# A hybrid attention and mixture-of-experts block on one core: two written orders of attention work replaced by two others

## The chip, the cores and the metric

The kernel runs on one core of one Trainium2 chip. The time is that of one execution on the device, in microseconds (us); several executions of the kernel before gave a median of 1522.29 us (1521.67 to 1523.18). Inside a core, TensorE multiplies and transposes, VectorE and ScalarE do elementwise work and copy results out of PSUM, GpSimd does small SBUF work, and SyncE issues most DMAs. In the profile they are PE (with PEld, its weight loads), DVE, ACT, POOL and SP.

## What is computed

Two layers on 256 tokens of width 1024. Each layer is an attention mixer with three kinds of heads, followed by a feed-forward part: a dense SwiGLU in layer 0, eight experts with two chosen for each token in layer 1.

```python
for layer in range(DEPTH):                                   # DEPTH = 2
    h = h + hybrid_mixer(rms_norm(h, attn_norm[layer]), ...)  # dsa, diff and mla heads, then @ w_out
    hn = rms_norm(h, ffn_norm[layer])
    if layer % 2 == 0:
        h = h + swiglu(hn, dense_w_gate[j], dense_w_up[j], dense_w_down[j])
    else:
        h = h + moe_ffn(hn, moe_router[j], moe_w_gate[j], moe_w_up[j], moe_w_down[j])
return rms_norm(h, final_norm)
```

In the mixer, "dsa" heads attend only to the 64 keys with the highest index score for each query. "diff" heads subtract one softmax from another, and "mla" heads work on keys and values that are expanded from a narrow latent.

## The kernel before

The 256 tokens are two tiles of 128 (t = 0 and 1). A float32 product is made of three passes over split operands: every weight part of 1024 columns is split into a high part by ScalarE (`split_hi`, L1293) and a low part by VectorE (`split_lo`, L1614), and TensorE runs high by high, high by low and low by high (`part_product`, L898).

The program has four stages after one another: attention of layer 0, `dense`, attention of layer 1, `experts`. In `dense` and `experts` the order is written in loops. In the two attention stages it comes from the two texts in `LISTS`. Each word is an item of work, and **every engine walks the same list** and issues its own share of each item (`attention` at L791 for GpSimd, L980 for TensorE, L1318 for ScalarE, L1754 for VectorE). An engine executes in the order in which it issues; between engines only semaphores hold. So a word's place decides what stands ahead of it on every engine that takes part. Nothing else plans the order: no costs, no due times.

The words that the later sections use:

- `X.t.i`, `OT.t.i`, `XF.t.i`: transposes of activations ahead of the input projections, the output projection and the feed-forward part. ScalarE and VectorE copy the result out, high and low.
- `SP.n`: the split of weight part n, four parts for each projection. Parts 0 to 19 belong to `PC`, `PA`, `PB`, `PI`, `PK`, parts 20 to 27 to the output projection, 28 to 30 to the first weights of the stage that follows. There are 7 buffers, so a split from part 7 on first waits until the projection that read part n - 7 is done (`part_free`, L473). A load into a ring slot waits until the slot's old parts are split.
- `PC`, `PA`, `PB`, `PI`, `PK` .t: input projections, 24 matmuls each. `C1`, `C2`, `CT`, `QC`, `KV`, `MQ`, `MK`: the mla latents' norm, their transposes and the expansion. `R.*`: rotary embedding on GpSimd.
- `U.kind.t.p`: logits of one pair of heads (TensorE, L973), their maximum (VectorE, L1718) and the exponential (ScalarE, L1414). For `U.idx`, the index heads, VectorE instead adds to the score (L1685, L1687). `CB`: the combination of a diff pair on VectorE (L1841 to L1844). `TP`, `O`: transposed probabilities, and the product with the values.
- `TK.t.r`: one of eight rounds that find the top 64 scores, all on VectorE (L1703, L1704), each on the result of the one before. `U.dsa` needs `TK.t.7`.
- `D1`, `D2`: the diff heads' norm. `WO.t.half`: the output projection, 24 matmuls, after all heads of tile t.
- `NF1`, `NF2`, `HS`, `RT`, `PL`, `GR` (layer 1): norm, split of the rows, router, places and the gather of rows for the experts. `GR.1.1` needs `HS.1.1`.
- `FL.n`: four transposes of the identity that nobody reads (`turn_identity`, L878). There are 16 in each list.

The list of layer 0 has 224 words, that of layer 1 has 240.

Of the kernel before, what the change touches and what calls it, by code (L numbers as in the profile page):

```python
# [38 lines left out]
C1.1 PA.0 PA.1 R.kr.0 CT.0 C2.1 SP.8 R.kr.1 FL.4 SP.9 QC.0.1 CT.1 SP.10 SP.11 KV.0.1 QC.0.0 KV.0.0 R.c.0 PB.0
MQ.0.0 MQ.0.1 MK.0.0 MK.0.1 KV.1.0 QC.1.1 QC.1.0 U.mla.0.3 SP.12 U.mla.0.2 KV.1.1 SP.13 R.c.1 CB.mla.0.3 PB.1  # L40
SP.14 MQ.1.1 SP.15 SP.16 R.a.0 MK.1.0 MK.1.1 CB.mla.0.2 U.mla.0.0 MQ.1.0 PI.0 SP.17 SP.18 SP.19 TP.mla.0.2
SP.20 SP.21 PI.1 TP.mla.0.3 PK.0 SP.22 U.mla.1.0 PK.1 R.i.0 KIT.0 SP.23 R.b.0 IT.0 O.mla.0.2 R.i.1 TP.mla.1.0
O.mla.0.3 R.a.1 U.idx.0.0 TP.mla.0.0 CB.mla.0.0 U.idx.0.1 U.idx.0.2 CB.mla.1.0 U.idx.0.3 BT.0 U.mla.1.2
U.mla.1.1 U.diff.0.2 KIT.1 CB.mla.1.2 CB.mla.1.1 FL.5 TK.0.0 O.mla.1.0 TK.0.1 O.mla.0.0 CB.diff.0.2 IT.1
TP.mla.1.2 U.diff.0.3 TP.mla.1.1 U.diff.0.1 TK.0.2 O.mla.1.2 CB.diff.0.3 TP.diff.0.2 U.mla.0.1 CB.diff.0.1
FL.7 O.mla.1.1 TK.0.3 TK.0.4 FL.2 TP.diff.0.3 O.diff.0.2 TK.0.5 U.idx.1.0 SP.24 R.b.1 AT.0 TP.diff.0.1
O.diff.0.3 CB.mla.0.1 U.idx.1.1 TP.mla.0.1 U.idx.1.2 U.idx.1.3 BT.1 U.diff.0.0 TK.0.6 U.diff.1.2 FL.12
CB.diff.0.0 O.diff.0.1 TK.1.0 CB.diff.1.2 O.mla.0.1 TK.0.7 TP.diff.0.0 U.dsa.0.0 U.dsa.0.1 O.diff.0.0 TK.1.1
TP.diff.1.2 CB.dsa.0.0 U.mla.1.3 D1.0 FL.13 TK.1.2 TP.dsa.0.0 FL.8 O.diff.1.2 FL.15 AT.1 TK.1.3 CB.mla.1.3
TK.1.4 CB.dsa.0.1 TP.dsa.0.1 U.diff.1.0 U.diff.1.1 O.dsa.0.0 FL.14 TP.mla.1.3 D2.0 CB.diff.1.0 U.diff.1.3  # L50
O.dsa.0.1 FL.3 CB.diff.1.1 TP.diff.1.0 O.mla.1.3 TK.1.5 OT.0.1 OT.0.0 TK.1.6 TP.diff.1.1 O.diff.1.0 TK.1.7
U.dsa.1.0 U.dsa.1.1 CB.diff.1.3 O.diff.1.1 WO.0.0 TP.diff.1.3 TP.dsa.1.0 O.diff.1.3 TP.dsa.1.1 D1.1 SP.25
# [6 lines left out]
TP.mla.0.1 U.mla.0.2 SP.15 CB.mla.0.1 MQ.1.1 TP.mla.0.0 SP.16 MK.1.1 PI.0 SP.17 SP.18 CB.mla.0.3 O.mla.0.1
U.mla.1.3 CB.mla.0.0 PI.1 TP.mla.0.3 SP.19 SP.20 SP.21 CB.mla.0.2 PK.0 SP.22 U.mla.1.0 PK.1 O.mla.0.0  # L60
O.mla.0.3 R.i.0 R.i.1 SP.23 CB.mla.1.3 TP.mla.1.3 R.b.0 TP.mla.0.2 IT.0 KIT.0 U.mla.1.2 O.mla.0.2 U.idx.0.0
TP.mla.1.0 O.mla.1.3 U.idx.0.1 TP.mla.1.2 KIT.1 U.idx.0.2 U.idx.0.3 TK.0.0 R.b.1 CB.mla.1.2 CB.mla.1.0 IT.1
# [2097 lines left out]
```

How the kernel before makes its waits and increments, by code:

```python
        def job(eng, key):  # L406
            eng.wait_ge(job_done, JOB[key] + 1)
            return work[JOB[key] % WBANKS]
# [1 line left out]
        def emptied(eng, key):  # L411
            eng.wait_ge(evacuated[JOB[key] % WBANKS], JOB[key] // WBANKS + 1)
# [7 lines left out]
        def arrived(eng, use, rounds=0):  # L421
            eng.wait_ge(slot_full[use % RING], rounds + 16 * (use // RING + 1))
# [50 lines left out]
        def part_free(eng, part, shift=0):  # L473
            for layer in range(DEPTH):
                i = (part - LAYER_PART[layer]) // 4
                if 0 <= i < len(SPLIT_SLOTS):
                    name = SPLIT_SLOTS[i]
                    keys = [(layer, name, t) if name in PROJ else (layer, "WO", t, int(name[2])) for t in range(T)]
                    eng.wait_ge(job_done, max(JOB[key] for key in keys) + 1)
                    return
            eng.wait_ge(part_used, shift + used_up(part))
# [76 lines left out]
        def roped_by(eng, layer, key):  # L559
            eng.wait_ge(roped, layer * len(ROPES[0]) + ROPES[layer].index(("R", *key)) + 1)
# [39 lines left out]
            def freed(use):  # L600
                if use in FREE:
                    sp.wait_ge(*FREE[use])
# [70 lines left out]
            def chunk_split(half, n):  # L673
                sp.wait_ge(lo_done, n * 4 + (first_part(half) + 4))
# [21 lines left out]
            def store(first):  # L697
                for t in range(T):
                    sp.wait_ge(out_ready, first + t + 1)
                    sp.dma_start(out[0, t * P:(t + 1) * P, :], final[:, t, :]).then_inc(stored, 16)
```

## Time and profile before

| | us |
|---|---|
| median of 3 executions | 1522.29 |
| the profiled execution | 1522.29 |
| its span, first to last instruction | 1520.5 |
| attention of layer 0, first projection to first dense product | 10.7 to 150 |
| attention of layer 1, first projection to first expert product | 389.2 to 539.2 |
| PE busy, share of the span | 1493.6 (98%) |
| DVE busy | 1255.1 (83%) |
| ACT busy | 1041.4 (68%) |

The busy time of PE counts pipelined matmuls and runs on through short waits, so the share is read together with the order of time. The granted clock is the share of TensorE's full clock that it was given; 1.00 is 2.4 GHz, and its other level is 0.5, 1.2 GHz. Over the span it was 0.992.

### The profile page before, as it was taken

What the parts mean: (1) busy time and instruction counts of PE and PEld (TensorE: products, weight loads), DVE (VectorE), ACT (ScalarE), POOL (GpSimd) and SP (SyncE); (2) the same over time, 40 slices, a digit from 0 to 9 for tenths busy, and PEclk for the clock granted to TensorE, in tenths of its full rate; (3) what the DMA queues carried; (4) which work ended last, traced back from release to release, by engine and by line L of the source; (5) the groups of instructions that cost most, each with busy time, mean ns of one, the idle gap of its engine ahead of it and who ended that gap; (6) DMA issues with size and microseconds to landing.
All of it is one profiled execution on the core that took longest, in us unless ns stands there. A gap on an engine that the chain in (4) does not pass through costs nothing.

```text
span 1520.5 us, 19069 instructions
## 1 busy us (share of the span) xinstructions
PE 1493.6 (98%) x7182; PEld 1245.2 (82%) x7182; DVE 1255.1 (83%) x1544; ACT 1041.4 (68%) x1362; POOL 98.1 (6%) x173
## 2 busy tenths in 40 slices
...
GB/s 283 202 56 56 241 189 199 171 212 127 125 202 57 57 282 384 387 363 364 351 362 364 359 363 363 365 363 377 342 370 362 365 367 365 362 371 375 363 371 107
DMA packets 181823, 431.11 MB, mean 284 GB/s; under 512 B 3937, under 2 KB 10465, under 8 KB 181729
## 3 DMA queue, kind: packets, MB, share of 16 engines
...
## 4 chain that ended last, share of the span: by engine, by line
PE 95%; DVE 2%; ACT 1%; issue 1%; DMA 0%; POOL 0%; POOLq 0%; ACTq 0%; SPq 0%; DVEq 0%
PE pair L903 51%; PE work L903 33%; PE work L875 3%; PE pair L973 2%; PE pair L875 2%; PE work L1047 1%; PE work L890 1%; PE work L1181 1%; DVE arena L1687 0%; PE work L1195 0%; PE work L1196 0%; ACT w_hi L1272 0%; DMA ring<-in_w_in 0%; DVE w_lo L1619 0%; DVE nmax L1718 0%
## 5 line engine op out<-in xcount | busy, mean ns | idle before, releaser
L1619 DVE TENSOR_TENSOR w_lo<-ring,w_hi 128x1024 fp32r<-128x1024 f32 (+3 forms) x810 | 961.6, 1213 | 191.2 <-ACT w_hi L1272 177.3
L1272 ACT ACTIVATE w_hi<-ring 128x1024 fp32r<-128x1024 f32 (+3 forms) x810 | 840.4, 1053 | 310.6 <-PE pair L903 140.3
L903 PE MATMUL pair<-w_hi,hnT_hi 128*128 128x512 f32 x672 | 265.1, 394 | 1.7 <-DVE hnT_lo L1986 0.9
L903 PE MATMUL pair<-w_hi,hnT_lo 128*128 128x512 f32 x672 | 262.0, 390 | 0.0
L903 PE MATMUL pair<-w_lo,hnT_hi 128*128 128x512 f32 x672 | 261.5, 389 | 0.0
L903 PE MATMUL work<-w_hi,hidT_hi 128*128 128x512 f32 x552 | 215.5, 390 | 2.6 <-DVE hidT_lo L1920 1.4
L903 PE MATMUL work<-w_lo,hidT_hi 128*128 128x512 f32 x552 | 214.9, 389 | 0.0
L903 PE MATMUL work<-w_hi,hidT_lo 128*128 128x512 f32 x552 | 214.8, 389 | 0.0
L903 PE MATMUL pair<-w_hi,xU_hi 128*128 128x512 f32 x448 | 177.1, 395 | 0.0
L903 PE MATMUL pair<-w_hi,xU_lo 128*128 128x512 f32 x448 | 174.8, 390 | 0.0
L903 PE MATMUL pair<-w_lo,xU_hi 128*128 128x512 f32 x448 | 174.3, 389 | 0.0
L903 PEld LDWEIGHTS pair<-w_hi,hnT_hi 128*128 128x128 f32 x672 | 126.2, 188 | 27.1 <-DVE hnT_lo L1636 1.2
L903 PEld LDWEIGHTS pair<-w_hi,hnT_lo 128*128 128x128 f32 x672 | 126.1, 188 | 26.8
L903 PEld LDWEIGHTS pair<-w_lo,hnT_hi 128*128 128x128 f32 x672 | 126.3, 188 | 25.2
L903 PEld LDWEIGHTS work<-w_hi,hidT_hi 128*128 128x128 f32 x552 | 103.7, 188 | 24.0 <-DVE hidT_lo L1920 1.6
L903 PEld LDWEIGHTS work<-w_hi,hidT_lo 128*128 128x128 f32 x552 | 103.6, 188 | 21.7
L903 PEld LDWEIGHTS work<-w_lo,hidT_hi 128*128 128x128 f32 x552 | 103.7, 188 | 20.9
L903 PEld LDWEIGHTS pair<-w_hi,xU_lo 128*128 128x128 f32 x448 | 84.1, 188 | 18.0
L903 PEld LDWEIGHTS pair<-w_lo,xU_hi 128*128 128x128 f32 x448 | 84.2, 188 | 16.7
L903 PEld LDWEIGHTS pair<-w_hi,xU_hi 128*128 128x128 f32 x448 | 84.1, 188 | 16.5
L903 PE MATMUL work<-w_hi,hnT_hi 128*128 128x512 f32 (+3 forms) x216 | 82.9, 384 | 2.4 <-DVE hnT_lo L1628 1.6
L903 PE MATMUL work<-w_hi,hnT_lo 128*128 128x512 f32 (+3 forms) x216 | 78.9, 365 | 0.0
...
## 6 DMA issues: line engine op xcount, KB each, us to landing
...
```

The source lines that it names most:

```text
L875: last = pe.transpose(b[0:n, i * P:(i + 1) * P], src, ident[:, :])
L890: last = pe.matmul(b[:, 0:n], lhs[k], rhs[k], start=(k == 0), stop=(k == len(rhs) - 1))
L903: mm = pe.matmul(b, lhs[x_part][k + kk], w[w_part][:, kk, :], start=(first and kk == 0 and i == 0), stop=(last and kk == 1 and i == 2))
L973: last = pe.matmul(S2[:, m, 0:nk], q, k, start=(m == 0 or kind != "diff"), stop=(kind != "diff"))
L1047: last = pe.matmul(b[:, 64 * m:64 * m + 64], pt[:, n % 2, m * (t + 1) + kb, :], v, start=(kb == 0), stop=(kb == t))
L1181: last = pe.matmul(banks[b][:, k * 2 * P:(k + 1) * 2 * P], v[:, c:c + P], sel[:, m // 2, :], start=(m == 0), stop=(m == 2 * T - 1))
L1272: return act.activation(o, i, ACT.Copy)
L1619: dve.tensor_tensor(lo, raw, hi.bitcast(F32), ALU.subtract).then_inc(lo_done, 1)
```

## The change

Both texts in `LISTS` are replaced. The set of words is the same in each list, so every engine executes the same work; only the order in which it is issued differs. No other line of the kernel changes. Of the diff, the first line of each list:

```diff
 LISTS = ("""
-N1.0 SP.0 FL.0 SP.1 X.0.0 X.0.1 SP.2 N1.1 SP.3 X.1.0 X.1.1 SP.4 SP.5 PC.0 SP.6 SP.7 AN PC.1 FL.1 C1.0 C2.0
...
+FL.12 N1.0 SP.0 X.0.1 X.0.0 SP.1 N1.1 SP.2 SP.3 X.1.0 FL.4 X.1.1 SP.4 SP.5 SP.6 AN SP.7 PC.0 C1.0 PC.1 C1.1
...
 """, """
-N1.0 X.0.0 X.0.1 SP.0 SP.1 N1.1 SP.2 SP.3 SP.4 SP.5 X.1.0 PC.0 X.1.1 C1.0 SP.6 C2.0 SP.7 PC.1 CT.0 PA.1 R.kr.1
...
+N1.0 X.0.0 X.0.1 N1.1 SP.0 SP.1 SP.2 SP.3 X.1.0 SP.4 SP.5 PC.0 X.1.1 SP.6 C1.0 C2.0 PC.1 C1.1 CT.0 SP.7 PA.0
...
```

The first place is TensorE in layer 0 after `PA`: the transposes of the latents (`CT`, 3 matmuls a tile), a filler (`FL`, 4 matmuls named `work<-ident`), and their expansion (`QC` with 384 columns, `KV` with 512). Before:

```order
L903 MATMUL work<-w_hi,hnT_lo 128x384
L875 MATMUL work<-ident,arena 128x128 x3
L875 MATMUL work<-ident 128x128 x4
L890 MATMUL work<-ring,arena 128x384 x2
L875 MATMUL work<-ident,arena 128x128 x3
L890 MATMUL work<-ring,arena 128x512
L890 MATMUL work<-ring,arena 128x384 x2
L890 MATMUL work<-ring,arena 128x512
```

The same place in the changed kernel:

```order
L903 MATMUL work<-w_hi,hnT_lo 128x384
L875 MATMUL work<-ident,arena 128x128 x6
L875 MATMUL work<-ident 128x128 x4
L890 MATMUL work<-ring,arena 128x384 x4
L890 MATMUL work<-ring,arena 128x512 x2
```

Both tiles' `CT` now stand together ahead of the expansion. One filler stands here in both; the other that stood between `PC.1` and `PA` has gone to the idle time before `PC.0`.

The second place is VectorE at the entrance of layer 1: the last add of the dense stage (L1964), splits of 832 and 768 columns (`SP.3` to `SP.6`), and the copies of `X.1.0` and `X.1.1` (L1636). Before:

```order
L1964 TENSOR_TENSOR h<-h,pair 128x512
L1604 TENSOR_TENSOR hn<-h,gain 128x512
L1590 TENSOR_SCALAR stat<-stat 128x1 x2
L1619 TENSOR_TENSOR w_lo<-ring,w_hi 128x832
L1619 TENSOR_TENSOR w_lo<-ring,w_hi 128x768 x2
L1636 TENSOR_TENSOR hnT_lo<-work,hnT_hi 128x4x128 x2
L1590 TENSOR_SCALAR cstat<-cstat 128x1 x2
L1619 TENSOR_TENSOR w_lo<-ring,w_hi 128x768
```

The same place in the changed kernel:

```order
L1964 TENSOR_TENSOR h<-h,pair 128x512
L1604 TENSOR_TENSOR hn<-h,gain 128x512
L1590 TENSOR_SCALAR stat<-stat 128x1 x2
L1619 TENSOR_TENSOR w_lo<-ring,w_hi 128x832
L1636 TENSOR_TENSOR hnT_lo<-work,hnT_hi 128x4x128
L1619 TENSOR_TENSOR w_lo<-ring,w_hi 128x768 x2
L1636 TENSOR_TENSOR hnT_lo<-work,hnT_hi 128x4x128
L1619 TENSOR_TENSOR w_lo<-ring,w_hi 128x768
```

The copy of `X.1.0` has moved ahead of two splits.

The third place is VectorE at the end of layer 1's attention: adds of the output projection (`WO`, L1880), the norm (L1590, L1766), splits (`SP.28` to `SP.30`, L1619), low parts of the rows (`HS`, L1897), copies of `XF` (L1640) and the start of the router (L1729). Before:

```order
L1880 TENSOR_TENSOR h<-h,work 128x512
L1590 TENSOR_SCALAR stat<-stat 128x1
L1766 TENSOR_TENSOR hn<-h,gain 128x1024
L1897 SCALAR_TENSOR_TENSOR hn_low<-hn,stat,hn_hi 128x512
L1619 TENSOR_TENSOR w_lo<-ring,w_hi 128x1024
L1880 TENSOR_TENSOR h<-h,work 128x512
L1619 TENSOR_TENSOR w_lo<-ring,w_hi 128x1024
L1897 SCALAR_TENSOR_TENSOR hn_low<-hn,stat,hn_hi 128x512
L1619 TENSOR_TENSOR w_lo<-ring,w_hi 128x1024
L1640 TENSOR_TENSOR arena<-work,gain_cols 128x4x128
L1880 TENSOR_TENSOR h<-h,work 128x512
L1640 TENSOR_TENSOR arena<-work,gain_cols 128x4x128
```

The same place in the changed kernel:

```order
L1880 TENSOR_TENSOR h<-h,work 128x512
L1590 TENSOR_SCALAR stat<-stat 128x1
L1619 TENSOR_TENSOR w_lo<-ring,w_hi 128x1024
L1766 TENSOR_TENSOR hn<-h,gain 128x1024
L1897 SCALAR_TENSOR_TENSOR hn_low<-hn,stat,hn_hi 128x512
L1880 TENSOR_TENSOR h<-h,work 128x512 x2
L1640 TENSOR_TENSOR arena<-work,gain_cols 128x4x128 x2
L1590 TENSOR_SCALAR stat<-stat 128x1
L1766 TENSOR_TENSOR hn<-h,gain 128x1024
L1640 TENSOR_TENSOR arena<-work,gain_cols 128x4x128
L1897 SCALAR_TENSOR_TENSOR hn_low<-hn,stat,hn_hi 128x512
L1729 TENSOR_SCALAR arena<-work,stat 128x8
```

Between the adds of `WO.1.0` and `WO.1.1` stood two splits and an `HS`; now the adds stand together, and this `HS` and two splits come later. The rows that follow in the changed kernel, down to the splits and the copies of the gathered rows (L1986):

```order
L1747 TENSOR_TENSOR sel<-arena 128x128 x2
L1752 TENSOR_TENSOR arena<-arena 128x16
L1619 TENSOR_TENSOR w_lo<-ring,w_hi 128x1024
L1897 SCALAR_TENSOR_TENSOR hn_low<-hn,stat,hn_hi 128x512
L1619 TENSOR_TENSOR w_lo<-ring,w_hi 128x1024 x2
L1986 TENSOR_TENSOR hnT_lo<-pair,hnT_hi 128x512 x4
```

`SP.29` stands ahead of `HS.1.1` and `SP.30` behind it; the second of the two splits in one row is the first of the experts' own.

## Rows read from the trace of the kernel before

**Rows 1.** Busy time of each engine in five stretches: start and length, then each engine's busy us.

```profile
core 0: us, PE busy (x) PEld busy (x) DVE busy (x) ACT busy (x) POOL busy (x), PEclk, DMA share, GB/s
11.00:75.00 64.00, 63.48 (x331) 53.94 (x330) 41.18 (x89) 36.94 (x79) 31.88 (x50) 1.00 0.64 235
76.00:119.00 43.00, 41.01 (x273) 33.79 (x272) 39.01 (x121) 27.95 (x100) 13.12 (x25) 0.92 0.14 50
...
389.00:455.00 66.00, 65.42 (x349) 56.43 (x347) 37.98 (x64) 35.73 (x77) 21.50 (x34) 1.00 0.52 182
455.00:498.00 43.00, 39.52 (x264) 33.15 (x263) 38.03 (x122) 25.42 (x88) 14.90 (x31) 0.88 0.16 59
...
539.00:1520.00 981.00, 969.74 (x4432) 803.88 (x4432) 899.55 (x887) 763.06 (x821) 2.36 (x4) 1.00 0.96 355
```

**Rows 2.** VectorE's waits, 76 to 124 us: line <- releaser: us in all, times, longest.

```profile
DVE nmax L1718 <- PE pair L976: 0.6, 2, 0.4
DVE arena L1685 <- ACT arena L1408: 0.5, 1, 0.5
```

**Rows 3.** TensorE in time, layer 0, around the latents: start us, us long, instruction [idle before].

```profile
29.30 0.60 PE L875 MATMUL work<-ident 128*128 128x128 f32 x4
30.20 1.53 PE L890 MATMUL work<-ring,arena 128*128 128x384 f32 x4 [0.30 <-DVE arena L1803]
```

**Rows 4.** TensorE in time, entrance of the dense stage.

```profile
147.98 1.91 PE L875 MATMUL work<-ident 128*128 128x128 f32 x16
...
157.03 0.47 PE L903 MATMUL pair<-w_hi,hnT_hi 128*128 128x512 f32 x1 [0.77 <-DVE hnT_lo L1636]
```

**Rows 5.** TensorE in time, entrance of layer 1.

```profile
394.11 0.60 PE L875 MATMUL work<-ident,hn 128*128 128x128 f32 x4
395.25 0.43 PE L903 MATMUL work<-w_hi,hnT_hi 128*128 128x416 f32 x1 [0.55 <-issue]
```

**Rows 6.** TensorE in time, layer 1, from the last projection to the first index head.

```profile
454.66 1.00 PE L1047 MATMUL work<-arena 128*128 128x64 f32 x8
...
456.70 1.03 PE L973 MATMUL pair<-arena 98*128 98x256 f32 x4
...
458.06 0.71 PE L973 MATMUL pair<-arena 64*128 64x128 f32 x4
```

**Rows 7.** VectorE in time, layer 1, the first index head and the wait ahead of it.

```profile
459.82 0.43 DVE L1685 TENSOR_SCALAR arena<-arena,wi 128x128 f32<-128x128 f32 x1 [1.17 <-ACT arena L1408]
```

**Rows 8.** VectorE's waits for TensorE, layer 1, 455 to 504 us.

```profile
DVE nmax L1718 <- PE pair L976: 0.9, 2, 0.7
```

**Rows 9.** TensorE in time, layer 1, after WO.0.0 and after WO.1.1.

```profile
503.65 1.03 PE L875 MATMUL work<-ident,arena 128*128 128x128 f32 x8
...
505.16 1.07 PE L1047 MATMUL work<-arena 128*128 128x64 f32 x8
...
509.01 1.07 PE L875 MATMUL work<-ident,hn 128*128 128x128 f32 x8
...
526.74 0.60 PE L875 MATMUL work<-ident,h 128*128 128x128 f32 x4
```

**Rows 10.** VectorE in time, from the last selection rounds of layer 1 to the experts.

```profile
497.18 0.69 DVE L1636 TENSOR_TENSOR hnT_lo<-work,hnT_hi 128x512 fp32r<-128x512 f32 x1
...
500.07 0.69 DVE L1718 TENSOR_REDUCE nmax<-pair 128x2 f32<-128x512 f32 x1
...
523.93 1.22 DVE L1619 TENSOR_TENSOR w_lo<-ring,w_hi 128x1024 fp32r<-128x1024 f32 x1
525.06 0.74 DVE L1897 SCALAR_TENSOR_TENSOR hn_low<-hn,stat,hn_hi 128x512 fp32r<-128x512 f32 x1
...
538.49 1.89 DVE L1986 TENSOR_TENSOR hnT_lo<-pair,hnT_hi 128x512 fp32r<-128x512 f32 x3 [0.94 <-ACT hnT_hi L1272]
```

**Rows 11.** TensorE in time, entrance of the experts.

```profile
539.23 0.50 PE L903 MATMUL pair<-w_hi,hnT_hi 128*128 128x512 f32 x1 [0.93 <-DVE hnT_lo L1986]
```

**Rows 12.** TensorE in time, the wait before its clock fell in layer 1.

```profile
472.58 0.30 PE L875 MATMUL work<-ident,arena 128*128 128x128 f32 x1 [1.73 <-DVE arena L1844]
```

More of the change, by code:

```diff
@@ L37 @@
 LISTS = ("""
-N1.0 SP.0 FL.0 SP.1 X.0.0 X.0.1 SP.2 N1.1 SP.3 X.1.0 X.1.1 SP.4 SP.5 PC.0 SP.6 SP.7 AN PC.1 FL.1 C1.0 C2.0
[L39 to L52, printed above, removed]
@@ L59 @@
[L59 to L62, printed above, removed]
-BT.0 U.idx.1.0 U.idx.1.1 U.idx.1.2 U.idx.1.3 R.a.1 U.diff.0.3 R.a.0 TK.0.1 O.mla.1.2 U.diff.0.2 AT.1
@@ new lines @@
+U.mla.1.2 TK.0.0 U.diff.0.2 O.mla.1.0 FL.11 TP.mla.1.1 R.a.1 TK.0.1 R.i.1 TK.0.2 TK.0.3 CB.mla.1.1 IT.1
+CB.diff.0.2 TP.mla.1.2 U.diff.0.3 R.b.1 U.mla.0.1 O.mla.1.1 KIT.1 TP.diff.0.2 U.diff.0.1 CB.mla.1.2
+CB.diff.0.3 O.mla.1.2 FL.3 TK.0.4 TP.diff.0.3 CB.diff.0.1 TK.0.5 O.diff.0.2 TP.mla.0.1 R.a.0 TK.0.6 FL.6
+O.diff.0.3 U.idx.1.0 U.idx.1.1 TP.diff.0.1 FL.15 U.idx.1.2 O.diff.0.1 U.idx.1.3 BT.1 AT.0 U.diff.0.0
+U.diff.1.2 TK.1.0 CB.mla.0.1 CB.diff.0.0 O.mla.0.1 TK.0.7 FL.8 CB.diff.1.2 SP.24 TP.diff.0.0 U.dsa.0.1
@@ new lines @@
+O.diff.0.0 U.dsa.0.0 TP.diff.1.2 TK.1.1 FL.14 U.mla.1.3 TK.1.2 CB.dsa.0.1 FL.5 FL.0 CB.mla.1.3 TP.dsa.0.1 D1.0
+U.diff.1.3 O.dsa.0.1 O.diff.1.2 FL.2 TK.1.3 TP.dsa.0.0 CB.diff.1.3 TP.mla.1.3 U.diff.1.0 D2.0 U.diff.1.1
+CB.dsa.0.0 CB.diff.1.0 O.mla.1.3 FL.13 O.dsa.0.0 TP.diff.1.3 CB.diff.1.1 TK.1.4 AT.1 TP.diff.1.0 OT.0.1 OT.0.0
+O.diff.1.3 O.diff.1.0 TK.1.5 TK.1.6 TK.1.7 U.dsa.1.0 TP.diff.1.1 CB.dsa.1.0 U.dsa.1.1 CB.dsa.1.1 WO.0.0
+TP.dsa.1.0 O.diff.1.1 D1.1 TP.dsa.1.1 SP.25 SP.26 O.dsa.1.0 SP.27 O.dsa.1.1 D2.1 WO.0.1 OT.1.1 OT.1.0 XF.0.1
```

37 lines of the change are left out of this document (23 added, 14 removed).

## The prediction, written before the changed kernel ran

> **What bounds the kernel now.** I read the busy time by stretches first, then the order of time on TensorE and VectorE at each stage's ends, then VectorE's waits in the two middles. The change touches only the two attention stages; `dense` and `experts` are loops, and in the experts TensorE is busy for 969.7 of 981 us at full clock [rows 1]. So I look for what moves the moment at which each of these two stages hands over.
>
> Each attention stage has three parts. In the projections (11 to 75 us, and 389 to 455) TensorE is busy 63.5 of 64 and 65.4 of 66 us, VectorE 41 and 38: TensorE bounds, and VectorE has room. In the middles (76 to 119 and 455 to 498) VectorE is busy 39.0 and 38.0 of 43 us, and ScalarE 28.0 and 25.4. TensorE shows 41.0 and 39.5, but at a granted clock of 0.92 and 0.88: with levels 1 and 0.5 that is 0.08 x 43 / 0.5 = 6.9 us and 0.12 x 43 / 0.5 = 10.3 us at half clock, filled with fillers and waits. So VectorE bounds the middles; what is left of 43 us are its waits and the small gaps between steps that use the result of the step before. In the last part (119 to 157, and 498 to 539) the four output projections fill TensorE, until the next stage waits for VectorE: the dense stage by 0.77 us for a copy [rows 4], the experts by 0.93 us [rows 11].
>
> **What the change does, part by part.** No instruction is added or removed; every term is a wait, or work that changes its side of a bound. Layer 0:
>
> 1. Projections, TensorE. A filler leaves the run of projections for a place where TensorE is idle. The row of four fillers gives 1.91 / 4 = 0.48 us each [rows 4]. With both `CT` ahead of the expansion, a transposing of the second tile and the remaining filler stand between `CT.0` and `QC`, which had waited 0.30 us for its copy [rows 3]. Both gone is -0.8; but ScalarE now has `SP.7` ahead of the copy of `PC.0`, and `SP.7` waits for `PC.1`, so the norm of the latents starts later. I take -0.6, bounds 0 and -0.8.
> 2. Middle. Item by item, VectorE has the same work between `PK.1` and the copy of `OT.0.0`, which releases `WO.0.0`: a `CB` has come in, one selection round has gone behind it. So only waits can go. They are 0.6 us for logits and 0.5 us for the index heads [rows 2], and the tail behind `WO.0.0` has its pieces in an order that leaves TensorE a little less to do. I take -1.0. Bounds: -1.7 if all of this goes; +1.5 if VectorE meets three more waits of the size seen there, because three selection rounds now run in one piece and are missing as cover two units later.
> 3. Entrance of `dense`. The list ends with two fillers where there were four: 0.96 us less on TensorE. I cost it at nothing: the first dense product runs, then TensorE waits at 157.03 for VectorE's copy [rows 4], and VectorE's chain from `WO.1.1` to that copy has kept its order. If that cover were not there it would be -0.96.
>
> Layer 0: -1.6.
>
> Layer 1:
>
> 4. Entrance. `PC.1` waited 0.55 us, and began 1.14 us after `PC.0` ended, of which one set of transposes explains 0.44 [rows 5]. Its input `X.1.0` now stands ahead of two splits. The wait goes: -0.7, bounds 0 and -0.8.
> 5. Up to the first index head. `U.mla.1.2`, two more `TP` and two more `O` now run within the projections, where TensorE bounds: about +2.0 us for TensorE (the unit alone is 0.9, the rest half-microsecond pieces). They leave the stretch from 454.66 to 458.06 [rows 6], 3.4 us long, of which 1.5 remain: -1.9. Together +0.1. VectorE waited 1.17 us there [rows 7], so it isn't hurt.
> 6. VectorE from that head to the release of `WO.0.0`. A third-last selection round and `U.mla.1.1` now come ahead of the copy of `OT`. From 497.18 to 500.07 there are one copy of 0.6 and two rounds, the second with a comparison [rows 10]: a plain round is about 1.0 us, the maximum of a unit 0.6. So +1.5, taken to +0.6, because the new order puts the diff units' maxima a step ahead of their combinations and the 0.9 us of waits for TensorE [rows 8] have other work in front of them. Bounds: -0.1 and +3.0, the second with twice the present waits on top.
> 7. From `WO.0.0` to `WO.0.1`. `TP.mla.1.1`, `O.mla.1.1` and a filler left this stretch, which begins at 503.65 and whose last transposes begin at 509.01 [rows 9]; they held 2.0 us. `O.mla.1.1` and a filler now stand before `WO.0.0` instead and delay it by 0.9. Net -1.1, bounds 0 and -2.0.
> 8. `XF.0.1` no longer stands between `WO.1.0` and `WO.1.1`: -0.4.
> 9. Tail. From 526.74, the end of `WO.1.1` [rows 9], to the first expert product at 539.23 [rows 11] it is 12.5 us, and VectorE is what it waits for. Two splits of 1.2 us and an `HS` of 0.7 [rows 10], which were done before `WO.1.1` ended, now come behind it and ahead of the copies of the gathered rows: 2.9 to 3.1 us. Of this the wait of 0.94 us before these copies [rows 10] and several short ones are cover. Queued behind are the router, `GR`, and the first products. I take +1.2, bounds 0 and +3.0.
>
> Layer 1: -0.7 + 0.1 + 0.6 - 1.1 - 0.4 + 1.2 = -0.3.
>
> **The sum.** -1.6 - 0.3 = -1.9 us. The profiled execution took 1522.29 us, 1.8 more than its span of 1520.5, and it is the median of the three runs, so the forecast is 1522.3 - 1.9 = 1520.4 us. About 0.2% (3.0 us) is what a measurement of this kernel can tell from no change, so this is "the same".
>
> **The rivals.**
>
> *A, forecast (45%)*: the small terms as above; its own range is 1518 to 1523.
>
> *B, the chain between the engines bounds the middles (26%)*, not VectorE's amount of work. For it: TensorE runs at half clock in exactly these stretches, and in layer 1 it stood 1.73 us for a combination on VectorE right before the clock fell [rows 12]. Against it: VectorE's waits in the two middles come to some 3 us in all. If the new order keeps TensorE ahead of VectorE, all waits of points 2 and 6 go, and of the 8.6 us that 17.2 us at half clock cost TensorE, say a third reaches VectorE: 1520.4 - 0.7 - 0.3 - 2.9 = 1516.5 us, faster.
>
> *C, the clock falls in the tail of layer 1 (16%)*. For it: before, 41 us with short waits end at full clock; now TensorE does 11 us of work in 13.7, in lumps: a wait for the copy of `XF.1.1`, one for `PL.0`, and one of 1 us or more for `HS.1.1` behind `SP.29`. In the middle of layer 1 the clock fell after waits like these [rows 12], and stayed down for about 10 us. Against it: fillers stand in this tail as well. If it falls as the experts begin, 10.3 us at half clock cost 5.1 us: 1520.4 + 5.1 = 1525.5 us. It decides once the waits of the tail together pass what was tolerated before 472.58, some 2 us.
>
> On this the Trainium skill speaks against the change: "TensorE: Matmul & The Clock Gate", "Part 1: The HAM clock gate", says that the throttled state is the default and that activity releases it, so taking fillers from the end of a list is a risk. The trace agrees that a wait preceded the fall in layer 1, and that with waits of 0.77 and 0.93 us at the two handovers the clock held.
>
> *D, nothing arrives (13%)*: in the middles a new wait replaces each old one, and the tail costs 2 instead of 1.2 us. 1522.3 us. For it: both orders hold the same work on the bounding engine.
>
> **How the numbers follow.** Faster by over 0.2%: B nearly whole (24%) and the lower edge of A (7%): 31%. Slower: C nearly whole (14%) and the upper edge of A and D (5%): 19%. Within 0.2%: 50%. The range reaches to B's and to C's value: 1515.5 to 1526 us.
>
> **What would show it.** Point 1: `PK.1` of layer 0 ends 0.4 to 0.8 us earlier than at 74.7 us. Point 2: `WO.0.0` starts within 2 us of 119.1. Point 3: TensorE waits about 1.7 us at the copy before its second dense tile. Point 4: no wait before `PC.1`. Point 9: from the end of `WO.1.1` to the first expert product 13 to 14.5 us, with a split right ahead of `HS.1.1`. B would show as a granted clock near 1 in the middles and both shorter by over 1.5 us; C as half clock across the first expert product. I am wrong in kind if a middle changes by more than 3 us, or if the experts themselves, from first product to last instruction, take other than the 981 us of before.

## The result: slower by 0.56%, outside the forecast's range

| | before | changed |
|---|---|---|
| median, us (executions) | 1521.98 (4) | 1530.52 (4) |
| lowest to highest, us | 1521.59 to 1523.18 | 1530.36 to 1532.62 |
| the profiled execution, its span | 1522.29, 1520.5 | 1529.41, 1527.6 |

The ratio is 1.0056, with a 95% interval from 1.0045 to 1.0068. The forecast was 1520.4 us, with a range up to 1526.0: wrong, and on the wrong side of no change. Of the 8.5 us between the medians the two profiled executions show 7.1: the one of before was 0.3 us above its median, the changed one 1.1 below its own.

The busy time in stretches of the changed kernel, in the columns of [rows 1], with the edges moved to the same events (first projection, first index head, copies of `OT`, first product of the next stage):

```profile
11.00:77.00 66.00, 63.76 (x330) 54.49 (x330) 44.84 (x89) 37.78 (x79) 25.17 (x43) 1.00 0.63 228
77.00:123.00 46.00, 43.94 (x288) 35.69 (x288) 40.14 (x127) 29.13 (x102) 16.67 (x34) 0.96 0.13 47
...
392.00:461.00 69.00, 68.67 (x369) 58.87 (x368) 39.25 (x68) 37.39 (x82) 26.80 (x41) 1.00 0.51 180
461.00:505.00 44.00, 39.58 (x259) 32.61 (x257) 36.01 (x120) 26.09 (x90) 12.26 (x24) 0.84 0.01 2
505.00:546.50 41.50, 39.08 (x244) 34.51 (x243) 32.10 (x67) 22.02 (x36) 5.47 (x9) 1.00 0.33 115
546.50:1527.00 980.50, 969.54 (x4432) 803.76 (x4432) 897.94 (x886) 760.58 (x818) 2.35 (x4) 1.00 0.96 355
```

The experts take their 981 us as before. All of the loss lies in the two attention stages. Their places in time:

| start of, us | before | changed | later by |
|---|---|---|---|
| layer 0: `PC.0` | 10.66 | 11.02 | 0.36 |
| copy of `PK.1` on VectorE | 74.70 | 76.14 | 1.44 |
| first index head on VectorE | 77.96 | 79.95 | 1.99 |
| `WO.0.0` / `WO.0.1` | 119.13 / 128.38 | 123.00 / 131.74 | 3.87 / 3.36 |
| second tile of `dense` | 157.03 | 160.35 | 3.32 |
| layer 1: `PC.0` / `PC.1` | 389.19 / 395.25 | 392.53 / 397.83 | 3.34 / 2.58 |
| `CT.0` | 399.86 | 403.21 | 3.35 |
| first index head on VectorE | 459.82 | 463.31 | 3.49 |
| `WO.0.0` | 498.13 | 505.26 | 7.13 |
| `WO.0.1` / `WO.1.1` | 509.83 / 521.19 | 515.77 / 526.74 | 5.94 / 5.55 |
| first expert product | 539.23 | 546.34 | 7.11 |

Four places make it up. The first is in layer 0's projections. On TensorE (start, length, instruction, idle before it and its releaser):

```profile
25.30 0.44 PE L903 MATMUL work<-w_hi,hnT_hi 128*128 128x384 f32 x1 [1.62 <-DVE w_lo L1619]
```

and on VectorE ahead of that split:

```profile
18.89 0.79 DVE L1648 CAST arena<-arena 128x2 f32<-128x2 int32 x1
19.72 0.57 DVE L1650 TENSOR_SCALAR arena<-arena 128x16 f32<-128x16 f32 x2
20.32 0.97 DVE L1590 TENSOR_SCALAR arena<-arena 128x32 f32<-128x32 f32 x1
21.32 0.55 DVE L1653 TENSOR_SCALAR arena<-arena 128x32 f32<-128x32 f32 x1
...
24.30 0.95 DVE L1619 TENSOR_TENSOR w_lo<-ring,w_hi 128x768 fp32r<-128x768 f32 x1
```

The rows from 18.89 us on are the item `AN`. The new list has `AN SP.7` where the old one had `SP.7 AN`, so the low split of part 7 stands behind sixteen small instructions, and `PA` waits 1.62 us for it.

The second and third are the middles. In layer 1 TensorE waits for a combination, then works at half clock through fillers, and VectorE waits for the dsa logits behind them:

```profile
476.83 0.45 PE L875 MATMUL work<-ident,arena 128*128 128x128 f32 x1 [3.07 <-DVE arena L1844]
...
486.72 1.97 PE L875 MATMUL work<-ident 128*128 128x128 f32 x8
488.48 0.85 PE L875 MATMUL work<-ident,arena 128*128 128x128 f32 x3
489.12 1.06 PE L875 MATMUL work<-ident 128*128 128x128 f32 x4
...
490.51 1.06 PE L875 MATMUL work<-ident 128*128 128x128 f32 x4
...
492.24 0.72 PE L973 MATMUL pair<-arena 64*128 64x128 f32 x8
```

```profile
493.05 0.42 DVE L1716 TENSOR_TENSOR arena<-pair,arena 128x256 f32<-128x256 f32 x1 [2.00 <-PE pair L973]
```

The wait of 3.07 us stands where [rows 12] had 1.73. Before, a second wait of 1.33 us for a combination followed it, so the waits of this kind come to 3.1 us in both kernels; what is new is that they stand in one piece, and that VectorE itself then waits: 4.1 us in all between its first index head and `WO.0.0`, where it was 1.3. The granted clock, cut at its changes (the same columns as the first table; the clock is the third value from the end):

```profile
106.02:109.42 3.40, 3.40 (x13) 2.92 (x14) 3.28 (x8) 1.62 (x8) 0.67 (x1) 0.50 0.00 0
474.66:481.48 6.82, 4.64 (x22) 4.34 (x22) 6.30 (x27) 2.62 (x12) 0.00 (x0) 0.50 0.00 0
481.49:484.89 3.40, 2.90 (x17) 2.15 (x17) 2.68 (x9) 1.95 (x8) 0.00 (x0) 1.00 0.00 0
484.90:491.72 6.82, 6.82 (x30) 5.88 (x30) 5.17 (x20) 3.63 (x15) 0.00 (x0) 0.50 0.03 5
```

In layer 1's middle it is half clock for 13.6 us, where before it was 10.2. The fourth place is the tail, whose entrance to the experts answers to [rows 11]:

```profile
546.34 0.50 PE L903 MATMUL pair<-w_hi,hnT_hi 128*128 128x512 f32 x1 [1.18 <-DVE hnT_lo L1986]
```

From the start of `WO.1.1` to this row it is 19.60 us, and was 18.04.

### The profile page after: what moved, and what is told of

Read it like the earlier page. It is cut to its first block, busy times and chain, and to the rows that moved or that the text cites. A ratio compares the mean times of both kernels' runs of the same rounds, so it can differ in the third digit from the quotient of the medians.

```text
span 1527.6 us, 19071 instructions
## 1 busy us (share of the span) xinstructions
PE 1496.9 (98%) x7182; PEld 1246.7 (82%) x7182; DVE 1255.2 (82%) x1544; ACT 1041.0 (68%) x1362; POOL 94.2 (6%) x173
## 4 chain that ended last, share of the span: by engine, by line
PE 94%; DVE 3%; ACT 1%; issue 1%; POOL 0%; POOLq 0%; DVEq 0%; ACTq 0%
PE pair L903 50%; PE work L903 32%; PE work L875 4%; PE pair L973 2%; PE pair L875 2%; PE work L1047 1%; PE work L890 1%; DVE w_lo L1619 1%; PE work L1181 1%; PE work L1195 0%; PE work L1196 0%; ACT w_hi L1272 0%; ACT arena L1380 0%; PE pair L976 0%; DVE hnT_lo L1628 0%
## 5 line engine op out<-in xcount | busy, mean ns | idle before, releaser
L1619 DVE TENSOR_TENSOR w_lo<-ring,w_hi 128x1024 fp32r<-128x1024 f32 (+3 forms) x810 | 961.6, 1215 | 193.4 <-ACT w_hi L1272 182.1
```

Of the source, the lines that this page charges most:

```text
L1619: dve.tensor_tensor(lo, raw, hi.bitcast(F32), ALU.subtract).then_inc(lo_done, 1)
```

## The experiments

Every kernel ran against the kernel before on the same chip, and there were three chips: one for E1 to E4, one for E5 to E9, one for E10 to E16. The kernel before had medians of 1521.8 to 1522.3 us on them. No run of the changed kernel is listed with them. All 24 executions of it on record have a median of 1530.4 us, but a difference from it, or between experiments of two groups, can hold a part that is the chip's. Diffs show words of a list only. "New list" is that of the changed kernel.

**E1 and E2: one list at a time.**

```diff
 E1:  LISTS = (new list of layer 0, old list of layer 1)
 E2:  LISTS = (old list of layer 0, new list of layer 1)
```

> The new order in layer 0 alone, the order of before in layer 1. Theory S (each list costs what its own stage shows in the two profiles, and the stages don't act on one another): the first projection of layer 1 starts 3.3 us later than before (392.5 against 389.2 us), layer 1 then takes the same 1131 us from there to the end of the span, and the time is 1522.0 + 3.3 = 1525.3 us. Theory K (the two lists act together, by the state in which one stage leaves TensorE's clock or the load queue): layer 1 changes too, and the time is not the sum; with the layer-1 run it would miss 8.5 us in all by more than 2 us.

> The order of before in layer 0, the new order in layer 1 alone. Theory S: layer 1 costs what its stage shows, 7.1 - 3.3 = 3.8 us by the profiles and up to 5.2 us by the medians (8.5 - 3.3), so 1525.8 to 1527.2 us; WO.0.0 starts 3.8 us later than before, the half clock in the middle of layer 1 lasts longer than 10.2 us, and from the end of WO.1.1 to the first expert product it is 14.2 us and not 12.5. Theory K: under 1524 or over 1529 us.

Measured: E1 1526.87 us (7 executions), ratio 1.0030 [1.0019, 1.0042]. E2 1525.64 us (11), ratio 1.0028 [1.0019, 1.0037]. The losses are 5.0 and 3.7 us, together 8.7 of 8.5: the times add up, so of S and K it is S that the medians bear out. The places are another matter. In E2's profile `WO.0.0` of layer 1 is only 2.4 us later against the stage's first projection, not 3.8. Its middle has 10.2 us at half clock, no more than before. The tail has 6.8 us at half clock and takes 20.3 us. And E1 is 1.6 us over the stage's own figure. Its profile, of the slowest of its seven executions, has the same list as the changed kernel's layer 0, and a `WO.0.0` that is 6.3 us late instead of 3.9. What differs is the clock:

```profile
102.75:112.98 10.23, 8.98 (x32) 7.41 (x33) 8.54 (x26) 5.09 (x20) 1.21 (x2) 0.50 0.00 1
```

10.2 us at half clock, where the changed kernel's profile had 3.4. So the same order costs different amounts in different executions, by 2.4 us at this place.

**E3 and E14: `AN` and `SP.7`.** E3 takes the suspect away from the changed kernel, E14 adds it to the kernel before.

```diff
 E3, layer 0, new list
-SP.6 AN SP.7 PC.0
+SP.6 SP.7 AN PC.0
 E14, layer 0, old list
-PC.0 SP.6 SP.7 AN PC.1
+PC.0 SP.6 AN SP.7 PC.1
```

> The changed kernel with the item AN put back behind SP.7 in layer 0, nothing else. Theory V (VectorE's low split of part 7 stood behind the sixteen small instructions of AN, and PA.1 waited 1.6 us for it): the wait of 1.62 us before PA's matmuls of the last part goes, the last projection of layer 0 ends 1.2 to 1.6 us earlier than at 76.0 us, and so does everything behind it: 1529 us, 1.5 less than the changed kernel's 1530.5. Rival R (AN has work whose users, the rotary embedding and the latents' norm, are then late by the same amount, or the projection waits for the next split instead): a new wait of 1 us or more before CT.0, QC or PB.1, and the end of the projections moves by under 0.5 us.

> The kernel before with AN ahead of SP.7 in layer 0, the words otherwise as they were. Theory V (the split of part 7 is late by VectorE's 3.9 us of small instructions, less its wait of 1.5 us for ScalarE, and PA waits): PE waits 1.0 to 2.4 us ahead of PA's last weight part, PK.1 ends 1.0 to 1.6 us later than before, and so does all behind it: 1523.2 us against 1522.1. Rival R (idle time of VectorE behind it absorbs the shift): PK.1 within 0.3 us, 1522.1 us.

Measured: E3 1529.49 us (5, from 1528.6 to 1532.5), 1.0 us under the changed kernel, which this scatter alone would not tell from nothing. The profile does: the wait is gone, and the copy of `PK.1` is 0.37 us late instead of 1.44, so 1.07 us are back (V had 1.2 to 1.6). E14 1526.07 us (9), ratio 1.0025 [1.0016, 1.0035]: 3.8 us for one word. In its profile `PA` waits, and the clock falls in the projections, where no other kernel here lost it:

```profile
26.12 0.44 PE L903 MATMUL work<-w_hi,hnT_hi 128*128 128x384 f32 x1 [2.26 <-DVE w_lo L1619]
```

```profile
26.85:30.25 3.40, 3.40 (x13) 3.40 (x12) 1.50 (x8) 0.73 (x2) 1.64 (x6) 0.50 0.86 295
```

The wait is 2.26 us, and 3.4 us at half clock are 1.7 us of work lost: 3.96, and `PB` starts 4.05 us later. All of it arrives at the end (4.2 us at `WO.1.1` of layer 1). Theory V is shown, and the price in the median was over three times the 1.1 us that it named.

**E4: the two dsa units next to each other.**

```diff
 E4, layer 0, new list
-U.dsa.1.0 TP.diff.1.1 CB.dsa.1.0 U.dsa.1.1 CB.dsa.1.1 WO.0.0
+U.dsa.1.0 CB.dsa.1.0 U.dsa.1.1 TP.diff.1.1 CB.dsa.1.1 WO.0.0
```

> The changed kernel with the item TP.diff.1.1 of layer 0 moved from between the two dsa units of tile 1 to behind them; nothing else. Theory P (two neighbouring units whose 64 rows lie in different halves of the array run side by side, and a transposition between them makes each run alone): the two units take 0.54 us each and not 1.06, and WO.0.0 of layer 0 starts 1.0 to 1.4 us after the copy of OT ends and not 1.6 with the transposition counted, i.e. 1.0 to 1.4 us earlier than at 123.0 us (1.04 for the units, 0.37 for the transposition that moves behind). Rival Q (the units run slowly because they wait for the buffer of the unit four before them, or for VectorE): they keep their 1.06 us each, and WO.0.0 moves by 0.4 us at most.

The changed kernel's TensorE (above) and E4's (below; line numbers in E1 to E4 are one lower):

```profile
120.52 1.13 PE L973 MATMUL pair<-arena 64*128 64x256 f32 x4
121.58 0.44 PE L875 MATMUL work<-ident,arena 128*128 128x128 f32 x2
121.95 1.13 PE L973 MATMUL pair<-arena 64*128 64x256 f32 x4
```

```profile
121.84 1.14 PE L972 MATMUL pair<-arena 64*128 64x256 f32 x8
122.91 0.44 PE L874 MATMUL work<-ident,arena 128*128 128x128 f32 x2
```

Eight matmuls take 1.14 us side by side, and four alone 1.13. Theory P holds for the units: from the copies of `OT` to `WO.0.0` it is 1.2 us less. But the median is 1531.88 us (5, from 1529.1 to 1533.5), no gain: `WO.0.1` is as far behind the copies of `OT` as in the changed kernel to 0.1 us. The transposed probabilities of the dsa units wait for VectorE's last selection round whatever `WO.0.0` does, and TensorE now waits 0.95 us there. In the profiles, then, the order of the two units is no cause of the loss.

**E5: four fillers fewer.**

```diff
 E5, layer 1, new list
-U.diff.1.0 FL.5 FL.1 AT.0 CB.diff.1.1 FL.8 O.diff.0.1 TK.1.3 TP.diff.0.0 FL.2
+U.diff.1.0 AT.0 CB.diff.1.1 O.diff.0.1 TK.1.3 TP.diff.0.0
```

> The changed kernel with four fillers of layer 1 left out (FL.5, FL.1, FL.8, FL.2: 16 transposes whose result nobody reads), those that stood at half clock between U.diff.1.0 and the dsa units of tile 0; nothing else. Theory F (fillers at half clock, 0.85 us each, were TensorE's path to the dsa units, for which VectorE waited 2.03 us): VectorE's wait before U.dsa.0.0 is under 0.3 us, WO.0.0 of layer 1 starts 1.7 to 2.1 us earlier than it would, and the median is 1528.5 us instead of 1530.5. Rival G (without them TensorE is idle there, the clock stays low longer, and what is saved in fillers is lost at half clock): half clock in the middle of layer 1 lasts 3.4 us or more longer than the 13.7 us of the changed kernel, and the median is within 0.7 us of 1530.5.

Measured: 1536.48 us (4), 6 us more than the changed kernel. F falls: VectorE still waits 1.6 us before the dsa logits. G has the direction of the clock right, but expected the median within 0.7 us:

```profile
485.63:506.10 20.47, 18.94 (x69) 14.26 (x69) 12.43 (x41) 10.47 (x43) 3.05 (x4) 0.50 0.02 3
```

Half clock began at the same item as in the changed kernel, 0.7 us later in time, and lasted 20.5 us instead of 6.8. `WO.0.0` comes 8.35 us later behind the first index head than before; in the changed kernel it was 3.65.

**E8, E9 and E16: fillers added where TensorE waited.**

```diff
 E8, new lists: layer 0, layer 1
+FL.16 FL.17 FL.18 TP.diff.0.0
+FL.16 FL.17 FL.18 FL.19 FL.20 TP.diff.0.3
 E9, old lists: layer 0, layer 1
+FL.16 U.diff.1.2 ... FL.17 FL.18 TP.diff.0.0
+FL.16 FL.17 FL.18 TP.diff.0.3 ... FL.19 FL.20 TP.diff.0.2
 E16, new list in layer 0 as in E8, old list in layer 1
```

> The changed kernel with eight fillers more (four transposes each that nobody reads), where TensorE stood waiting for a combination on VectorE: three ahead of TP.diff.0.0 in layer 0 (it waited 1.54 us) and five ahead of TP.diff.0.3 in layer 1 (3.07 us). Theory H (it is the idle time before these transposes that makes the clock fall, and the fall that makes the middles long): half clock in the two middles together is under 10 us (the changed kernel's profile had 17.1), both middles are 1 to 2 us shorter, and the median is 1527 to 1528.5 us. Rival I (the clock falls for the low activity of the whole middle, whatever stands in one gap): half clock of 13 us or more, the fillers run at 0.85 us, and the median is 1530 to 1533 us.

> The kernel before with fillers added where TensorE waited in its middles: one ahead of U.diff.1.2 (0.87 us) and two ahead of TP.diff.0.0 (1.12 us) in layer 0, three ahead of TP.diff.0.3 (1.73 us) and two ahead of TP.diff.0.2 (1.33 us) in layer 1. Theory H: half clock in the middles falls from 17.1 us to under 10, and the time to 1520 us or less. Rival I: half clock is as long as before or longer, the added fillers run at 0.85 us and come out behind the waits, and the time is 1522 to 1524 us. Rival V (VectorE bounds the middles, whatever the clock): half clock falls, but the time stays within 0.7 us of 1521.9.

> The new order in layer 0 with three fillers ahead of TP.diff.0.0, the order of before in layer 1. Theory O (the order itself costs 3.4 to 3.9 us in layer 0, the clock the rest of the 4.9 us that the layer cost without these fillers): most executions have no half clock in layer 0's middle, layer 1's first projection starts 3.4 to 3.9 us later than before, and the median is 1522.1 + 3.7 = 1525.8 us with the lowest at 1525.2. Theory H (the clock is most of it): with the clock up, the layer costs under 2.5 us, 1524.5 us or less.

Measured: E8 1529.81 us (6, from 1528.4 to 1541.3). E9 1522.56 us (11): eight at 1521.3 to 1522.9 and three at 1530.0 to 1530.4. E16 1531.53 us (5, from 1528.0 to 1533.9). The profile of E8 has no half clock in layer 0's middle at all, that of E9 none in layer 1's, but a long one in layer 0's:

```profile
77.00:124.00 47.00, 44.29 (x302) 36.08 (x303) 41.13 (x130) 29.63 (x102) 17.09 (x35) 1.00 0.13 48
```

```profile
107.56:124.61 17.05, 17.05 (x65) 13.53 (x64) 9.38 (x29) 6.58 (x24) 2.33 (x3) 0.50 0.00 1
455.00:505.00 50.00, 45.83 (x332) 39.47 (x332) 43.47 (x129) 29.87 (x96) 17.28 (x34) 1.00 0.24 85
```

In E8 neither H's time nor I's clock came. H's first half can come true (the clock stays up), but it brings nothing to the kernel before: executions of E9 with a mean clock of 0.996 to 0.999 take as long as those of the kernel before at 0.992 to 0.994. That is E9's rival V, that VectorE bounds the old middles whatever the clock, and it holds for eight of the eleven executions, whose median is 1522.1 us. The other three lose 8 us, which none of the theories had; in the profile, one of them, `WO.0.0` of layer 0 comes 7.4 us later behind the first index head than before, with the 17 us at half clock in between. E16, meant as quiet ground, was worse than E1 by 4.7 us (on another chip, each against its own kernel before), and no theory there holds either. Theory O keeps one thing: with the clock up throughout layer 0's middle (E8), `WO.0.0` is still 1.9 us later behind the first index head than before. The three fillers didn't make this: the transposes behind them still waited 0.23 us for VectorE. That much is the order.

**E7 and E10: the tail of layer 1.**

```diff
 E7, layer 1, new list
-HS.0.0 WO.1.0 WO.1.1 XF.0.1 FL.10 XF.1.0 NF1.1 NF2.1 XF.1.1 HS.0.1 RT.0 ... PL.1 SP.29 GR.0.0 ... GR.1.1 SP.30
+HS.0.0 WO.1.0 SP.29 HS.0.1 SP.30 WO.1.1 XF.0.1 FL.10 XF.1.0 NF1.1 NF2.1 XF.1.1 RT.0 ... PL.1 GR.0.0 ... GR.1.1
 E10, layer 1: everything behind WO.0.1 as in the old list, with one filler more
```

> The changed kernel with SP.29, HS.0.1 and SP.30 of layer 1 put back between WO.1.0 and WO.1.1, nothing else. Theory T (VectorE's two splits and the HS behind WO.1.1 lengthen the tail, and in some executions the clock falls there for the waits that they make): from the end of WO.1.1 to the first expert product 12.5 to 12.8 us instead of 14.2; no half clock in the tail; the executions of 1532 us and more are gone, and the median is 1528.6 us. Rival U (the split of parts 28 to 30 isn't what the tail waits for: the router's chain through RT and PL is): the tail keeps at least 13.7 us, the median is 1530 us or more, and slow tails at a lower mean clock remain.

> The changed kernel, with all of layer 1 behind WO.0.1 in the order of before (one filler more, as there). Theory C (the order of the tail sets its length, and in the changed kernel its waits also let the clock fall in some executions): from the end of WO.1.1 to the first expert product 12.5 us and not 14.2, WO.1.1 0.35 us later for XF.0.1, no half clock between WO.1.1 and the first expert products, no execution over 1531.5 us, and the median 1530.5 - 1.7 + 0.4 = 1529.2 us, or 1528.7 if the falls of the clock weigh in the median. Rival L (the tail is sensitive to what the middle leaves, such as a part not yet split or a load not yet landed: SP.24 to SP.27 are later in this list): the tail keeps over 13.5 us, or the clock falls in it as in the run with three words put back, and the median is 1530 to 1539 us.

Measured: E7 1538.89 us (4), 8.4 us more than the changed kernel. E10 1529.20 us (5), none over 1530.3, and 18.07 us from `WO.1.1` to the first expert product. In E7 theory T fell. U's figures hold, but not its reason: what TensorE waits for is VectorE's add of `WO.1.1`, ahead of the router. E10 is as theory C expected, in the tail and in the median. In E7, VectorE:

```profile
528.03 1.23 DVE L1619 TENSOR_TENSOR w_lo<-ring,w_hi 128x1024 fp32r<-128x1024 f32 x1 [4.48 <-ACT w_hi L1272]
...
535.39 0.68 DVE L1880 TENSOR_TENSOR h<-h,work 128x512 f32<-128x512 f32 x1
```

and TensorE:

```profile
536.21 1.09 PE L875 MATMUL work<-ident,h 128*128 128x128 f32 x4 [2.62 <-DVE h L1880]
```

```profile
536.14:553.20 17.06, 16.64 (x78) 16.61 (x79) 8.92 (x29) 6.82 (x9) 1.46 (x1) 0.50 0.16 48
```

In the new list `SP.28` stands ahead of `NF2.0` and `HS.0.0`, and VectorE waits 4.5 us for its high part, which ScalarE can't write before a buffer is free. In the changed kernel it waits as long (4.47 us), but the adds of `WO.1.1` follow sooner there. VectorE is late by that, and three more items ahead of the adds of `WO.1.1` make TensorE wait 2.62 us for them; 17 us at half clock follow, across the first expert product. That is rival C of the prediction, in full size. In E10, with the whole old tail, `SP.28` stands behind `HS.0.0`, and the same three words cost nothing. VectorE has done the norm and the low parts by the time the high part comes:

```profile
528.22 1.23 DVE L1619 TENSOR_TENSOR w_lo<-ring,w_hi 128x1024 fp32r<-128x1024 f32 x1 [1.31 <-ACT w_hi L1272]
```

So the new tail costs 19.60 - 18.07 = 1.5 us, of which 0.4 come back because `XF.0.1` no longer stands ahead of `WO.1.1`, and it is a set that can't be taken word by word. In E2, E4, E5 and E11, which have the new tail, the profiled execution lost the clock there for 6.8 to 10.2 us, and the stretch took 20.3 to 21.9 us: C happens to the changed order too, in some executions, for 0.7 to 2.3 us more.

**E11 and E15: VectorE's work ahead of the copies of `OT`.** E11 also has E3's and E8's edits.

```diff
 E11, layer 1, new list
-TK.1.5 TK.1.6 O.diff.1.3 TP.mla.1.1 OT.0.1 O.diff.1.2 OT.0.0 FL.7
+TK.1.5 O.diff.1.3 TP.mla.1.1 OT.0.1 O.diff.1.2 OT.0.0 TK.1.6 FL.7
 E15, layer 1, old list
-OT.0.0 TK.1.5 OT.0.1 TP.diff.1.3 TK.1.6 TK.1.7 U.mla.1.1
+OT.0.0 TK.1.5 TK.1.6 U.mla.1.1 OT.0.1 TP.diff.1.3 TK.1.7
```

> The changed kernel with three repairs: AN behind SP.7 in layer 0 (alone it gave 1.07 us at the end of the projections), the eight fillers in TensorE's waits (alone they gave 0.7 us in the median and left layer 1's middle 2.0 us shorter in the profile), and the selection round TK.1.6 of layer 1 behind the copies of OT instead of ahead. Theory W (VectorE's work ahead of the copies sets the middle once the clock is up): the copies of OT in layer 1 come 1.0 us earlier than with the fillers alone, WO.0.0 of layer 1 starts 5.73 - 1.1 - 1.0 = 3.6 us later than in the kernel before, and the median is 1529.8 - 1.1 - 1.0 = 1527.7 us. Rival X (the time between WO.0.0 and WO.0.1 absorbs it, as VectorE has the same work ahead of OT.1): WO.0.0 comes earlier but WO.0.1 does not, and the median is 1528.7 us.

> The kernel before with the selection round TK.1.6 and the unit U.mla.1.1 of layer 1 moved ahead of OT.0.1. Theory W (work of VectorE ahead of the copies of OT delays the output projection by its own length, and part of that comes back between WO.0.0 and WO.0.1, where the same work is then missing): WO.0.0 starts 1.3 to 1.7 us later than at 498.1 us, WO.0.1 0 to 1.0 us later, and the median is 1522.6 us. Rival Z (all of it arrives at the end): WO.0.1 as late as WO.0.0, 1523.7 us.

Measured: E11 1528.08 us (9, from 1526.5 to 1540.6). From the first index head to `WO.0.0` of layer 1 it is 0.7 us less than in E8, not 1.0, and 0.6 of it is left at `WO.0.1`. W is near in the profile (0.7 of 1.0 us); with this scatter the median can't tell W's 1527.7 us from X's 1528.7. E15 1529.07 us (5), ratio 1.0042 [1.0029, 1.0056]: 6.8 us, where 0.4 to 1.5 were expected. The chain is short. VectorE gives the maximum of `U.mla.1.1` at 498.12 us, behind the moved round; ScalarE's exponential waits for it, with the copy of `OT.0.1` queued behind it; and TensorE waits for ScalarE:

```profile
498.85 0.47 ACT L1414 ACTIVATE arena<-pair,nmax 128x256 f32<-128x256 f32 x1 [3.66 <-DVE nmax L1718]
...
499.76 0.59 ACT L1272 ACTIVATE hnT_hi<-work 128x512 fp32r<-128x512 f32 x1
```

```profile
500.77 1.09 PE L1047 MATMUL work<-arena 128*128 128x64 f32 x4 [4.31 <-ACT arena L1272]
```

```profile
500.45:507.27 6.82, 6.50 (x20) 4.93 (x21) 4.68 (x10) 1.97 (x8) 0.00 (x0) 0.50 0.00 1
```

`WO.0.0` is 5.7 us late and none of it comes back. Both theories had counted 1.6 us of VectorE's work, and neither the ScalarE queue between nor the clock.

**E12 and E13: can the kernel before be bettered?**

```diff
 E12, layer 1, old list
-SP.3 SP.4 SP.5 X.1.0 PC.0
+SP.3 X.1.0 SP.4 SP.5 PC.0
 E13: the same, and in layer 0
-X.1.0 X.1.1 SP.4 SP.5 PC.0 SP.6 SP.7 AN PC.1 FL.1 C1.0
+X.1.0 FL.1 X.1.1 SP.4 SP.5 PC.0 SP.6 SP.7 AN PC.1 C1.0
```

> The kernel before with one word moved: X.1.0 of layer 1 ahead of SP.4 and SP.5. Theory E (point 4 of the prediction alone): the 0.55 us wait before PC.1 goes, everything behind it in layer 1 starts 0.7 to 0.8 us earlier, and the median is 1521.2 us against 1521.9. Rival N (VectorE's splits SP.6 and SP.7, late by a copy, are waited for at PA instead, or VectorE bounds the middle whatever the entrance does): a wait of 0.4 us or more before PA, or WO.0.0 of layer 1 within 0.2 us of before, and 1521.9 us.

> The same, and in layer 0 the filler FL.1 moved from between PC.1 and PA to the idle time of TensorE ahead of X.1.1. Theory E: another 0.44 us in layer 0 by the filler's row (0.48 us each at full clock), which arrives at WO.0.0 and at the end: 1520.8 us. Rival N: PA then waits 0.4 us for VectorE's split of part 7, or VectorE in the middle gives it back, and it takes as long as the kernel with one word moved.

Measured: 1521.35 us (11) and 1521.68 us (11) against 1522.12, both with a ratio of 0.9996 [0.9987, 1.0005]. Not told apart from the kernel before, so no better version is claimed. In E12's profile, counted from `PC.0` of layer 1, `PC.1` starts 0.80 us earlier, but from `PA` on only 0.4 are left, and 0.2 at `WO.0.0`, which is rival N's figure. E13's further 0.4 us don't show in the median.

## Why the prediction was wrong, point by point

The step that failed is the price of a moved item. In its central values the forecast took VectorE's work as the bound of both middles and let waits only go away (points 2 and 6: -1.0 and +0.6 us); measured are +1.9 by `WO.0.1` and +3.65, because new waits and half clock came. And one row of the change in the projections, `AN` ahead of `SP.7`, was missed, which made TensorE wait 1.62 us. The late norm and splits at the end (point 9) were seen, and only their size was a little low.

**Point 1** (projections of layer 0, -0.6 forecast): measured +1.44. What it missed is a row of the change, `AN` ahead of `SP.7` on VectorE, though it named `SP.7` on ScalarE. The terms that it counted came only in part, as E3 shows, which is without the missed one: `PI.0` starts 0.57 us earlier than before, but between `PI.0` and `PK.1` the new order takes 1.0 us more, where `U.mla.0.2`, `U.mla.0.3` and `TP.mla.0.0` have moved in. From the start of `PC.0` to that of `PK.1` it is 59.8 us in E3, 60.05 before and 61.15 in the changed kernel. And `PC.0` itself starts 0.36 us later, which the forecast had not priced.

**Point 2** (middle, -1.0, bounds -1.7 and +1.5): from `PK.1` to `WO.0.0` +2.4 in the profile, of which 0.5 come back by `WO.0.1`. 0.55 us come ahead of the first index head, 1.1 are waits on VectorE behind it. The sign was wrong, and so was the bound of three more waits (+1.5): E8 has +2.4 with no half clock at all. The same list gave, from the first index head to `WO.0.0`, compared with before: 1.9 us with no half clock (E8) and with 3.4 us of it (the changed kernel), 2.8 and 3.3 with 6.8 us (E5, E10), 4.2 with 10.2 us (E1), though 3.5 with 3.4 us that came later (E16).

**Point 3** (entrance of `dense`, nothing): right. The two fillers' 0.9 us went into the wait for the copy, 1.65 us instead of the 0.77 of [rows 4].

**Point 4** (-0.7): the wait went and `PC.1` began 0.76 us earlier against the stage, but nothing was left by `CT.0`. `PC.1` also reads `X.1.1`, whose copy had not moved.

**Point 5** (+0.1): measured +0.14 from `CT.0` to the first index head.

**Point 6** (+0.6, bounds -0.1 and +3.0): the largest miss, 3.65 us. Its work term of 1.5 is in the profile as forecast (`TK.1.6` 0.98 us, `U.mla.1.1` 0.60). I then took it down for waits that would vanish; instead VectorE's waits grew by 2.8 us, 2.0 of them at the dsa logits. With the clock better (E8: 6.8 us at half clock) the stretch is 1.7 us longer than before, with 10.2 us (E2, E10) 2.4, with 13.6 us (changed) 3.65, with 27.3 us (E5) 8.35.

**Points 7 and 8** (-1.1 and -0.4): measured -1.2 and -0.4. **Point 9** (+1.2): measured +1.56, and E10 takes it back.

So the sum by profile is +7.1 against -1.9. (The working has two slips that change nothing here. Rival B takes another 0.3 us off point 6, where the forecast had already taken off all 0.9 us of waits. And the range, said to reach to B's and C's values of 1516.5 and 1525.5, goes 1.0 and 0.5 us past them.) Of the 9.0 us missed, 2.0 are point 1, 2.9 point 2 (up to `WO.0.1`), 0.75 points 4 and 5, 3.05 point 6 and 0.35 point 9.

How much is the clock? In all, the profiled execution had as much half clock as that of before, 17.1 us, less of it in layer 0 and more in layer 1. E8's profile is the one with little, 6.8 us, and its first expert product is 5.7 us late, of which 0.6 came with a later start than the changed kernel's. So about 5.1 us are there with 6.8 us at half clock, and 7.1 - 5.1 = 2.0 us came with the 6.8 us more of it in layer 1's middle. How much of the 5.1 hangs on the half clock that is left, no run shows. The 1.1 us from the changed kernel's profiled execution to its median may be more half clock: the mean clocks suggest it (0.993 at 1529.2 to 1530.0 us, 0.988 and 0.989 at 1531 to 1534), and no profile shows it.

The old order is another matter. From the first index head to `WO.0.0` of layer 1 it takes 38.1 to 38.4 us, whether none of this is at half clock (E9), 6.8 us (E13) or 10.2 us (the kernel before, E1, E12, E14 and E16). With the new list it is 40.7 us at 10.2 us (E2, E10) and 41.6 to 42.0 at 13.6 (E3, E4, E7 and the changed kernel). So the first 10 us at half clock were free in the old order, and in the new one 2.4 us are lost at the same amount.

The weighing had a fault of its own. Forecast A took the half clock as given, and in the middles it priced the edits at the busy time that they move, with waits as something that can vanish. Rival B used the clock for a gain alone, rival C put its loss into the tail alone. What the runs show is a loss that is a multiple of the wait: a few items moved make a wait on TensorE (2.26 us in E14, 4.31 in E15, 2.62 in E7), half clock follows for 3.4, 6.8 and 17 us, and E14 and E15 are 3.8 and 6.8 us slower than the kernel before, E7 8.4 us slower than the changed one. The prediction cited the Trainium skill, "TensorE: Matmul & The Clock Gate", "Part 1: The HAM clock gate", for the risk in taking fillers away, as activity releases the throttle. E5 bears it out in the middle of layer 1: with four fillers gone, half clock lasted 13.6 us longer. What the runs leave open is which execution falls for how long: E9 and E16 show the same kernel at either end.
